# Summing eight chunks of a modulation weight on VectorE instead of multiplying them on TensorE, in a one-core transformer block

## The reference

```
mod_x = split(silu(c)     @ w_mod + b_mod, 6)     # w_mod is 1024 x 6144
mod_c = split(silu(c_ctx) @ w_mod + b_mod, 6)
hx = modulate(rmsnorm(x),   mod_x[0], mod_x[1])
hc = modulate(rmsnorm(ctx), mod_c[0], mod_c[1])
s_f, s_b = context_states(hc, w_in, ret_log_decay)
x = x + mod_x[2] * token_mixers(hx, ..., s_f, s_b)     # retention, short convolution, gates
x = x + mod_x[5] * hier_moe(modulate(rmsnorm(x), mod_x[3], mod_x[4]), ...)   # 32 experts
return rmsnorm(x)
```

## Time and profile before

| | us |
|---|---|
| median of 3 runs | 1205.27 |
| lowest, highest | 1200.65, 1205.41 |
| profiled execution, its span | 1207.0 |
| PE busy in the span | 1099.4 (91%) |
| DVE busy | 891.4 (74%) |
| ACT busy | 721.8 (60%) |

### The profile page before, as it was taken

How to read it: one execution, slowest core, us unless ns; L and a number is a source line. 1 busy time by engine, 2 the same in 40 slices (tenths; PEclk the granted TensorE clock), 3 DMA queues, 4 the chain that set the end, 5 groups by cost and what they waited for, 6 DMA issues and landing times.

```text
span 1207.0 us, 16558 instructions
## 1 busy us (share of the span) xinstructions
PE 1099.4 (91%) x6355; PEld 932.1 (77%) x6355; DVE 891.4 (74%) x849; ACT 721.8 (60%) x688; POOL 17.5 (1%) x37
## 2 busy tenths in 40 slices
PE   2798999999999999997989999999999999999983
PEld 2396878888778899995678778787788877878772
DVE  3865355384365657557559998999999899999974
ACT  4733435353354433445258878887888788878762
POOL 1000000000000000001000000000000000000000
PEclk9898999999999999998589999999999999999996
DMA  9943126272344645546338999999999999999950
GB/s 330 329 141 140 70 93 256 71 256 94 140 164 160 236 145 204 190 176 204 138 140 299 345 348 335 354 360 352 345 355 361 355 334 359 345 364 330 363 214 37
DMA packets 126803, 296.70 MB, mean 246 GB/s; under 512 B 3068, under 2 KB 3292, under 8 KB 126756
## 3 DMA queue, kind: packets, MB, share of 16 engines
q1 hardware_dynamic: 125156, 292.66, 67.3%
q0 software_dynamic: 1600, 3.38, 1.0%
HBM read 294.92 MB, written 1.05 MB: 245 GB/s over the span
## 4 chain that ended last, share of the span: by engine, by line
PE 59%; DVE 12%; DMA 11%; issue 10%; ACT 8%; DVEq 1%; SPq 0%; ACTq 0%
DMA raw<-in_expert_w 10%; PE ps L507 8%; PE ps L508 8%; PE ps L509 8%; DVE lo L295 7%; ACT hi L288 6%; PE ps L519 3%; PE ps L520 3%; PE ps L521 3%; PE ps L728 3%; PE ps L729 3%; PE ps L749 3%; PE ps L707 2%; PE ps L627 2%; PE ps L770 2%
## 5 line engine op out<-in xcount | busy, mean ns | idle before, releaser
L295 DVE TENSOR_TENSOR lo<-raw,hi 128x2048 fp32r<-128x2048 f32 x276 | 619.9, 2288 | 125.6 <-ACT hi L288 124.1
L288 ACT ACTIVATE hi<-raw 128x2048 fp32r<-128x2048 f32 x276 | 517.4, 1917 | 179.4 <-PE ps L509 105.5
L728 PE MATMUL ps<-hi,xg 128*128 128x512 f32 x512 | 201.7, 394 | 3.6 <-DVE actp L1388 1.9
L729 PE MATMUL ps<-lo,xg 128*128 128x512 f32 x512 | 201.0, 393 | 0.0
L507 PE MATMUL ps<-hxh,hi 128*128 128x256 f32 x576 | 166.1, 288 | 5.8 <-DVE hxl L1121 4.5
L508 PE MATMUL ps<-hxl,hi 128*128 128x256 f32 x576 | 164.3, 285 | 0.0
L509 PE MATMUL ps<-hxh,lo 128*128 128x256 f32 x576 | 164.3, 285 | 0.0
L770 PE MATMUL ps<-hi,actp 128*128 128x512 f32 x256 | 107.9, 422 | 17.4 <-issue 13.7
L728 PEld LDWEIGHTS ps<-hi,xg 128*128 128x128 f32 x512 | 97.1, 190 | 26.2 <-issue 4.0
L507 PEld LDWEIGHTS ps<-hxh,hi 128*128 128x128 f32 x576 | 111.7, 194 | 6.8 <-issue 5.0
L729 PEld LDWEIGHTS ps<-lo,xg 128*128 128x128 f32 x512 | 97.1, 190 | 20.0
(11 more groups left out here) (246 smaller groups left out, 1492.9 us busy)
## 6 DMA issues: line engine op xcount, KB each, us to landing
raw<-in_expert_w SPq DMA_DIRECT2D x96, 2048.0 KB, 9.7
raw<-in_w_in SPq DMA_DIRECT2D x22, 2048.0 KB, 7.9
raw<-in_w_mod SPq DMA_DIRECT2D x12, 2048.0 KB, 9.6
raw<-in_w_ret_o SPq DMA_DIRECT2D x4, 2048.0 KB, 7.8
raw<-in_w_conv_o SPq DMA_DIRECT2D x2, 2048.0 KB, 8.2
raw<-in_w_out SPq DMA_DIRECT2D x2, 2048.0 KB, 8.5
xtok<-in_x SPq DMA_DIRECT2D x1, 1024.0 KB, 7.3
xtok<-in_ctx SPq DMA_DIRECT2D x1, 1024.0 KB, 10.4
```

What stands on the lines that cost most here:

```text
L288: eng.activation(hi[part_slot][:, k, :], raw[raw_slot][:, k, :], ACT.Copy).then_inc(hi_done, 1)
L295: eng.tensor_tensor(lo[part_slot][:, k, :], raw[raw_slot][:, k, :], hi[part_slot][:, k, :], ALU.subtract).then_inc(lo_done, 1)
L728: pe.matmul(ps[:, 4 + half, :], xg[:, s, k, :], hi[slot][:, k, :], start=(k == 0), stop=False)
L729: last = pe.matmul(ps[:, 4 + half, :], xg[:, s, k, :], lo[slot][:, k, :], start=False, stop=(k == 7))
```

## The change

Chunks 4 to 11 of the modulation are no longer split and multiplied. DVE reads the raw chunk itself: it multiplies row block 0 by its column of silu(c), and adds blocks 1 to 7 in place, each scaled by its column, in fp32 (eight chained instructions, each waiting for the one before). That leaves 128 partitions x 512 in `macc`, of which there are two. One fp32 matmul of PE with a column of ones then sums over the partitions. ACT copies one row instead of four, and `mstack` holds 8 + 8 rows instead of 32 + 8. The slots of `hi` and `lo`, and the count of halves, go by the chunks that are still split (34 instead of 42); the raw slots and the order of the loads stay. A load whose raw slot held a summed chunk waits for DVE's sum.

```
+def summed(step):
+    return step[0] == "M" and step[1] >= 4
+
+SPLITS = [s for s in CHUNKS if not summed(s)]
...
+for _m, _ahead_of in ((4, ("K", 0)), (5, ("V", 1)), (6, ("RO", 0)), (7, ("T", 1)), (8, ("RO", 1)), (9, ("V", 3)),
+                      (10, ("RO", 2)), (11, ("T", 3))):
+    DVE_STEPS.remove(("M", _m))
+    DVE_STEPS.insert(DVE_STEPS.index(_ahead_of), ("M", _m))
...
             for j, (kind, n) in enumerate(CHUNKS):          # SP
                 if j >= RAW:
-                    sp.wait_ge(lo_done, 2 * (j - RAW) + 2)
+                    of = CHUNKS[j - RAW]
+                    if summed(of):
+                        sp.wait_ge(dve_step, dve_count(of))
+                    else:
+                        sp.wait_ge(lo_done, 2 * SPLITS.index(of) + 2)
...
+                elif summed(step):                          # PE
...
+                    after(act=act_reader, dve=dve_reader)
+                    after(act=("M", j - 1), dve=step)
+                    pe.wait_ge(made, 1)
+                    last = pe.matmul(ps[0:1, M_BANK.get(j, 6), :], onecol[:, :], macc[:, j % 2, :], start=True, stop=True)
...
-                    done(act.activation(mrow[0:4, j % 2 if j < 4 else 0, :], ps[0:4, M_BANK.get(j, 6), :], ACT.Copy))
+                    rows = 4 if j < 4 else 1
+                    done(act.activation(mrow[0:rows, j % 2 if j < 4 else 0, :], ps[0:rows, M_BANK.get(j, 6), :], ACT.Copy))
...
+                elif summed(step):                          # DVE
+                    n = CHUNKS.index(step)
+                    V.wait_ge(landed[n % RAW], 16 * (n // RAW + 1))
+                    if j >= 6:
+                        pe_at(("M", j - 2))
+                    acc, part = macc[:, j % 2, :], raw[n % RAW]
+                    L(V.tensor_scalar(acc, part[:, 0, :], csilu[:, 0:1], None, ALU.mult))
+                    for k in range(1, KT - 1):
+                        L(V.scalar_tensor_tensor(acc, part[:, k, :], csilu[:, k:k + 1], acc, ALU.mult, ALU.add))
+                    done(V.scalar_tensor_tensor(acc, part[:, KT - 1, :], csilu[:, KT - 1:KT], acc, ALU.mult, ALU.add))
```

More of the change, by code:

```diff
@@ L69 @@
 assert C0 % RAW == 0
+def summed(step):
+    return step[0] == "M" and step[1] >= 4
+SPLITS = [s for s in CHUNKS if not summed(s)]
+S0 = len(SPLITS)
+assert not any(summed(s) for s in CHUNKS[-RAW:])
 ACT_KINDS = ("XT", "M", "K", "V", "S", "G", "PV", "T", "CH", "CB", "GA", "GB", "MA", "HT", "LG")
@@ L77, in pe_count @@
 def pe_count(step):
-    return sum(s[0] not in CHUNKED for s in STEPS[:STEPS.index(step) + 1])
+    return sum(s not in SPLITS for s in STEPS[:STEPS.index(step) + 1])
 def act_count(step):
@@ L88 @@
 DVE_STEPS.insert(DVE_STEPS.index(("T", 1)) + 1, ("K", 1))
+for _m, _ahead_of in ((4, ("K", 0)), (5, ("V", 1)), (6, ("RO", 0)), (7, ("T", 1)), (8, ("RO", 1)), (9, ("V", 3)),
+                      (10, ("RO", 2)), (11, ("T", 3))):
+    DVE_STEPS.remove(("M", _m))
+    DVE_STEPS.insert(DVE_STEPS.index(_ahead_of), ("M", _m))
 def dve_count(step):
-    return sum(s[0] in DVE_KINDS for s in DVE_STEPS[:DVE_STEPS.index(step) + 1])
+    return sum(s[0] in DVE_KINDS or summed(s) for s in DVE_STEPS[:DVE_STEPS.index(step) + 1])
 def block_kernel(nc, x, c, ctx_in, c_ctx, w_mod, b_mod, norm1_w, norm2_w, w_in, ret_log_decay, ret_gn_w,
@@ L276, in wait_pe, with raw_of @@
         def wait_pe(eng, step):
-            if step[0] in CHUNKED:
-                eng.wait_ge(half_used, 2 * CHUNKS.index(step) + 2)
+            if step in SPLITS:
+                eng.wait_ge(half_used, 2 * SPLITS.index(step) + 2)
             else:
                 eng.wait_ge(pe_step, pe_count(step))
+        def raw_of(j):
+            n = CHUNKS.index(SPLITS[j]) if j < S0 else C0 + j - S0
+            return n % RAW, 16 * (n // RAW + 1)
         def split_hi(eng, raw_slot, lands, part_slot, halves=(0, 1)):
@@ L341, in number @@
         def number(r, place):
-            return C0 + 3 * NE * r + 6 * place[0] + place[1]
+            return S0 + 3 * NE * r + 6 * place[0] + place[1]
         def lands_of(r, place):
@@ L347, in expert_slot_free @@
         def expert_slot_free(eng, r, place):
-            eng.wait_ge(chunk_done, number(r, place) - C0 - HLB + 1)
+            eng.wait_ge(chunk_done, number(r, place) - S0 - HLB + 1)
         def split_ahead(r, place):
-            return isinstance(r, int) and isinstance(place[0], int) and number(r, place) - C0 < HLB
+            return isinstance(r, int) and isinstance(place[0], int) and number(r, place) - S0 < HLB
         def expert_hi(eng, r, place):
@@ L553, in _ @@
                     pe.wait_ge(silu_parts, 1)
[L554 to L559, removed]
+                    bank = 6
                     for k in rows_of(8):
@@ L583, in _ @@
                     after(act=act_reader, dve=dve_reader)
-                    last = pe.matmul(ps[:, bank, :], selm[:, j - 4:j - 3].broadcast_to([40, P]), mstack[:, :], start=True, stop=True)
+                    last = pe.matmul(ps[:, bank, :], selm[:, j - 4:j - 3].broadcast_to([16, P]), mstack[:, :], start=True, stop=True)
                 elif kind == "K":
@@ L688, in _ @@
                     last = pe.matmul(ps[:, 5, 2 * NE:3 * NE], ones[:, :], mask[:, 1, :], start=False, stop=True)
-                if kind not in CHUNKED:
+                if step not in SPLITS:
                     last.then_inc(pe_step, 1)
@@ L941, in _ @@
                                        bias=stat[:, b:b + 1]).then_inc(roots, 1)
-                    splits.up_to(2 * C0 + 5)
+                    splits.up_to(2 * S0 + 5)
                     preload(ACT.Exp)
@@ L946, in _ @@
                 elif kind == "LG":
-                    splits.up_to(2 * C0 + 6)
+                    splits.up_to(2 * S0 + 6)
                     act.wait_ge(logit_ready, 1)
@@ L1248, in _ @@
                 elif kind == "HT":
-                    splits.up_to(2 * C0 + 4)
+                    splits.up_to(2 * S0 + 4)
                     V.wait_ge(roots, 3)
```

42 lines of the change are left out of this document (25 added, 17 removed).

## The result

| | before | after |
|---|---|---|
| median of 20 executions each, us | 1204.47 | 1211.48 |
| ratio, 95% interval | | 1.0071 [1.0051, 1.0092] |
| profiled execution, its span | 1207.0 | 1215.4 |
| its PE / DVE / ACT busy | 1099.4 / 891.4 / 721.8 | 1085.9 / 901.3 / 691.2 |

What follows compares the result with a forecast made beforehand. PE was taken to bound 120 to 560 us, with the removed 26 us of PE time becoming waiting. Waits +1.0 and clock +8.4 gave +9.4 us, 1207.0 to 1216.4 profiled; median 1214.7, range 1204 to 1221.

Steps and rivals of the forecast that it cites:

- M4: Ahead of V0 on PE: DVE's idle time hides the sum, V0 starts unchanged, PE waits 6.3 us, not 3.0; worth 0.
- M5: Ahead of RO0: the sum delays G1's load and split, then v_sb, so RO0 starts 0.3 us later.
- M6, M10: Between RO0's or RO2's end and S1 or S3: PE goes on sooner, -1.15 us each, -2.3 together.
- M7, M8: T1 to Q1: DVE is the bound, four halves out (8.9 us), 10.1 in; +0.55 us for both.
- M9: Ahead of RO2, with V3 and G3: same course as M5, +0.3 us.
- M11: Ahead of RO3: DVE's sum stands before T3, so ytl and RO3 come later; +2.15 us.
- clock: PE falls to half clock behind new waits at RO0, RO2, RO3 and, as a half, Q1: 3.5 x 2.4 = +8.4 us.
- The sum: On DVE, per chunk: one scaling at 0.48 us, seven scaled additions at 0.69; 5.55 us, bounds 4.9 to 6.0.
- The load: A load waiting for DVE's sum, such as G1's, is issued and landed 8.2 us after the sum ends.
- The ones-matmul: On PE, per summed chunk: taken as 0.45 us, from 0.23 to 0.62.
- The rival with a steady clock: Waits as forecast, but the clock stays up or its falls are hidden: 1206.3 us; chance 0.17.
- the faster one: DVE is nowhere late, so PE steps start when their next releaser allows: -8.8 us, 1196.5; 1179 if PE's time counts whole; chance 0.08.

Runs made afterwards that it cites:

- the second one: The changed kernel again, unaltered, timed a second time against the kernel before: 1211.22 us, ratio 1.0116.
- 1: Changed kernel plus 11, 7, 5, 9 and 8 unused fp32 matmuls in PE's new waits, M11's ones-matmul 6 times, against the kernel before: 1218.55 us, ratio 1.012.
- 3: Changed kernel with five sums moved earlier on DVE and six unused matmuls ahead of four ones-matmuls, against the kernel before: 1203.76 us, ratio 1.0007.
- 2: Changed kernel with five of DVE's eight sums moved earlier, no extra PE work, against the kernel before: 1201.73 us, ratio 0.9981.
- 4: Kernel before, but chunks 4 to 11 multiply only their lo part on PE (values wrong), against the kernel before: 1204.25 us, ratio 1.0028.
- 5: Changed kernel with five sums moved earlier and three unused matmuls ahead of four ones-matmuls, against the kernel before: 1194.91 us, ratio 0.995.
- 7: As 5, plus five unused matmuls at M4 and eight ahead of the second norm's transposes (HT), against the kernel before: 1189.29 us, ratio 0.9907.
- 6: Changed kernel, sums unmoved, with 5, 3, 2, 4 and 4 unused matmuls, M11's ones-matmul 3 times, against the kernel before: 1209.21 us, ratio 1.0083.
- 11: The kernel of 6 timed again, against the kernel before: 1212.94 us, ratio 1.0126; 1.0014 of the changed kernel.
- 12: Kernel before with only eight unused matmuls ahead of the second norm's transposes (HT), against the kernel before: 1199.98 us, ratio 1.0005.

## Why the prediction was right, step by step

The forecast put +1.0 us on waits and +8.4 on the clock. The places, from the profiled execution of after and, in brackets, from the second one; each is a distance between two starts on PE, with that of before taken off:

| step | predicted | measured |
|---|---|---|
| M4 (V0's start) | 0 | +0.65 (-0.59) |
| M5: T0 to RO0 | +0.3 | +1.40 (+1.50) |
| M6, M10: RO's end to S1, S3 | -1.15 each | -1.08 each (the same) |
| M7, M8: T1 to Q1 | +0.55 | +1.70 (+1.51) |
| M9: T2 to RO2 | +0.3 | +0.44 (+0.13) |
| M11: T3 to RO3 | +2.15 | +2.51 (+2.51) |
| clock: RO0, Q1, RO2, RO3 longer | 3.5 x 2.4 = 8.4 | 2.04 + 1.60 + 1.78 + 1.65 = 7.1 (7.2) |

The mechanism is right at every place and so is the sign, but that the total comes so close (+9.4 forecast, +8.4 in the profiles, +7.0 and +11.2 in the two pairs of medians) is in part luck: the waits were put 2.9 us too low, the clock 1.3 too high, and 3.4 us came back behind RO3, which the forecast had at nothing.

V0 starts a little later in the one execution and sooner in the other, but 6.73 us behind K0's last matmul before, after and in the second execution, so M4's 0 holds to the hundredth; V0's wait grew to 5.78 where 6.3 was said, the ones-matmul being longer. Without V0 the waits come to +3.9 (+3.5), where +1.0 was said; with the clock's 7.1 that is 11.0, and with V0 11.6 of the 11.8 us at the conv projection. Of these, 1.9 came back ahead of the logits (the table above), 1.2 in the routing behind them, where the clock's falls lay otherwise, and 0.3 in the experts: 8.4 at the end. The prediction had taken all behind RO3 to keep its distances.

The mechanism held at each place. **M7 and M8**, the chain on DVE from K1's last row, to be read against the earlier trace rows:

```profile
238.74 2.29 DVE L316 TENSOR_TENSOR lo<-raw,hi 128x2048 fp32r<-128x2048 f32 x1 [9.15 <-ACT hi L309]
240.95 1.66 DVE L1237 SCALAR_TENSOR_TENSOR g_sb<-ps,cols,g_sb 128x256 f32<-128x256 f32 x4
...
249.28 1.23 DVE L1188 TENSOR_TENSOR k_sb<-k_sb,q_sb 128x1024 f32<-128x1024 f32 x1
250.54 0.48 DVE L1129 TENSOR_SCALAR macc<-raw,csilu 128x512 f32<-128x512 f32 x1
251.06 4.69 DVE L1131 SCALAR_TENSOR_TENSOR macc<-raw,csilu,macc 128x512 f32<-128x512 f32 x6
...
256.58 4.49 DVE L316 TENSOR_TENSOR lo<-raw,hi 128x2048 fp32r<-128x2048 f32 x2
260.99 2.28 DVE L1248 TENSOR_TENSOR racc<-racc,ps 128x2048 f32<-128x2048 f32 x1
...
263.32 0.39 PE L534 MATMUL ps<-hxh,hi 128*128 128x256 f32 x1 [3.04 <-DVE racc L1248]
```

The addition `racc` follows the splits without a gap, though RO1 had ended at 259.33: DVE is the bound, and RO1's own fall of the clock is hidden, as the prediction had it. The split of Q1's half ended at 241.03, which is 237.8 on the old scale (T1 lies 3.2 us later here) where 236.2 was said, and held T1's first row back by some 0.8; M8's sum and the splits took 0.3 more than said. **M6** and **M11**:

```profile
191.67 2.29 DVE L1246 COPY racc<-ps 128x2048 f32<-128x2048 f32 x1 [1.45 <-PE ps L536]
...
194.10 0.67 PE L646 MATMUL ps<-q_sb,k_sb 128*128 128x256 f32 x2 [1.53 <-DVE racc L1246]
```

```profile
397.18 0.48 DVE L1129 TENSOR_SCALAR macc<-raw,csilu 128x512 f32<-128x512 f32 x1
397.69 4.69 DVE L1131 SCALAR_TENSOR_TENSOR macc<-raw,csilu,macc 128x512 f32<-128x512 f32 x6
402.42 0.75 DVE L1132 SCALAR_TENSOR_TENSOR macc<-raw,csilu,macc 128x512 f32<-128x512 f32 x1
403.20 1.66 DVE L1237 SCALAR_TENSOR_TENSOR g_sb<-ps,cols,g_sb 128x256 f32<-128x256 f32 x4
...
407.37 0.55 PE L534 MATMUL ps<-yth,hi 128*128 128x256 f32 x1 [2.93 <-ACT mrow L888]
```

T3's first row on DVE stands right behind the sum, as forecast.

Four terms had a wrong size:
- **The sum.** 0.69 us a row was taken and 0.75 measured; in the chain 4.69 for six, so 0.785 with the step between them. A whole sum lasts 6.0, the upper of the two bounds, 0.45 more than taken. The row taken reads one operand from the accumulator memory (`ps`), this one reads both from SBUF; the prediction knew this, yet set 0.69 against the page as the trace's figure for SBUF to SBUF, which it is not.
- **The load.** The 8.2 of the median was taken; G1's landed some 9.0 behind the sum's end (159.10 to 168.1), Q1's 9.4 (227.3 to 236.7). With the sum's 0.45 that is M5's excess, and what held T1. G3's took 8.1 (331.3 to 339.4), which is why M9 stayed near its forecast.
- **The clock.** A fall that PE had to pay cost 1.6 to 2.0 here and not 2.4, since part of each low stretch lies over the wait that brought it (RO0's from 175.7 to 182.5, with RO0 starting at 177.81). There were five behind V0's, four of them to be paid. Over all runs a fall took 1.3 to 2.8.
- **The ones-matmul.** It is recorded as two matmuls and holds PE for 0.87, not 0.45. I had read the four rows of L584 as four matmuls; they were two. It costs nothing here, since it lies in a wait, but every filler of 1 and 3 came out too long by it.

The rival with a steady clock failed (13.8 us for RO0's product), and so did the faster one: it needed sums under 3 us, or, as 2 shows, another place for them. The Trainium skill, "TensorE: Matmul & The Clock Gate", section "HAM oscillation", says that a PE which waits between bursts starts the next one at the half rate; the traces bear it out, in 1 by restoring the clock with work of no use, and in 4 by losing it with nothing but less work.

## What to carry to other kernels

Work on the busiest engine that fills its waits is worth nothing when removed, until what those waits end on is moved too. Ask of each removed piece what the next instruction waits for, and of each added one which load and which copy stand behind it in its queue: here the same eight sums cost 0.7 to 1.2% in one order and nothing in another. Where TensorE has less to do, a few matmuls of no use that end ahead of the releaser keep its clock; they must be sized by a measured row, as too many cost more than the falls (1 and 3). They paid in the median only where the sums stood in their right place (5 and 7), not in the changed kernel itself (6 and 11) nor ahead of `HT` (12).

## What the runs showed of the hardware that was not expected

- A scaled addition of 512 fp32 columns with both tensors in SBUF takes 0.75 us, with one in the accumulator memory 0.69. The Trainium skill, "VectorE: DVE Perf Modes", section on the TRN2 errata, would give 0.594 by its table (an estimate from that page), and says itself that this row of the table comes out short for a single instruction; the trace agrees with that, by 0.16.
- An fp32 matmul of one stationary column over 512 columns is recorded twice, and holds PE 0.87 us at full clock: 40 of them are 80 in number 1.

```profile
L586 PE MATMUL ps<-rope,onecol x80: 590/592/593, 171.7 to 410.2; 128*1 128x512 f32 x80
```

- These matmuls of one column kept the clock at 1.00 (2.4 GHz) in 1, 3, 5 and 7, as the wide ones do; the next item has the one case in which they did not.
- Behind which waits the clock fell to 0.50 (1.2 GHz), from 95 to 440 us: behind each of 3.25 to 6.3 us in all these kernels, and behind the three of 2.94 to 3.04 ahead of Q1; behind the one of 3.02 ahead of V0 in the kernel before and not in number 12; behind 2.07 in number 11, where 5.3 us of one-column matmuls lay ahead of it, and not behind 2.00 in number 6 with the same ahead, nor behind 2.01 in the kernel before. Waits of up to 1.74 us had none. Ahead of RO3 after the change, 3.89 us and, behind the ones-matmul, 2.93 brought one fall between them.
- The same code behind the logits took 618.0 to 631.3 us from one execution to another, and V0's start behind the same code up to M4 lay from 98.2 to 102.4.
